# Expert retrieval of a streaming encoder step: separate gathers of U and V rows, two of nine tiles by a dense pass

## What is computed

```python
q = (xb @ w_query).reshape(PEER_BLOCK, PEER_HEADS, 2, D_HALF)
s = jnp.einsum('thpd,hpkd->thpk', q, sub_keys)
sv, si = lax.top_k(s, PEER_TOPK)                      # 16 of 128, twice per head
cand = sv[:, :, 0, :, None] + sv[:, :, 1, None, :]    # sums of pairs
cidx = si[:, :, 0, :, None] * N_KEYS + si[:, :, 1, None, :]
...
fv, fi = lax.top_k(cand, PEER_TOPK)                   # 16 experts per head
eidx = jnp.take_along_axis(cidx, fi, axis=-1)
g = jax.nn.softmax(fv, axis=-1)
a = jnp.einsum('thkd,td->thk', expert_u[eidx], xb)
w = g * jax.nn.gelu(a, approximate=False)
return jnp.einsum('thk,thkd->td', w, expert_v[eidx])
```

## Time and profile before

| what | value |
|---|---|
| median of 3 runs | 3683.47 us (3682.42 to 3684.99) |
| span of the profiled execution | 3684.3 us |
| PE busy | 3158.2 us, 86% |
| DVE busy | 2311.1 us, 63% |
| POOL busy | 1110.6 us, 30% |
| ACT busy | 719.1 us, 20% |
| gather queue | 1208.03 MB, 79.4% of 16 engines |

### The profile page before, as it was taken

The page is one execution under the profiler, slowest core; times in us unless marked ns, Lnnn a source line. Parts: engine busy times, 40 slices in busy tenths (PEclk is TensorE's granted clock), DMA queues, the critical chain, the costliest instruction groups (busy, mean ns, idle before and its releaser), DMA issues.

```text
span 3684.3 us, 48012 instructions
## 1 busy us (share of the span) xinstructions
PE 3158.2 (86%) x17895; PEld 1389.9 (38%) x17895; DVE 2311.1 (63%) x6107; ACT 719.1 (20%) x2373; POOL 1110.6 (30%) x1177
## 2 busy tenths in 40 slices
PE   6999999889888878988887898889788888977776
PEld 3545556634334324423432343344234334422222
DVE  1333343867757866775776677677667757765444
ACT  2434434311111111111111111111111111111111
POOL 0000000033333333333333333333333333333332
PEclk8999999799999999999999999999999999999999
DMA  5000114299999999999999999999999999999997
GB/s 217 24 29 23 35 34 169 91 401 421 421 421 419 418 414 417 413 414 420 415 414 420 416 414 415 417 418 416 412 417 416 416 416 418 413 414 420 419 418 326
DMA packets 192682, 1275.60 MB, mean 346 GB/s; under 512 B 21056, under 2 KB 24768, under 8 KB 44608
## 3 DMA queue, kind: packets, MB, share of 16 engines
q0 software_dynamic: 165888, 1208.03, 79.4%
q1 hardware_dynamic: 26560, 64.49, 4.9%
HBM read 1260.12 MB, written 12.32 MB: 345 GB/s over the span
## 4 chain that ended last, share of the span: by engine, by line
DMA 46%; PE 35%; DVE 9%; issue 5%; POOL 4%; ACT 1%; SPq 0%; DVEq 0%; POOLq 0%; ACTq 0%
DMA arena<-in_experts,arena 45%; PE PS L1353 10%; PE PS L1182 8%; PE PS L1367 7%; POOL arena L651 4%; DVE arena L976 4%; PE PS L1276 3%; PE PS L1166 2%; PE PS L1399 2%; PE PS L1265 1%; PE PS L1225 1%; DVE arena L1051 1%; DVE arena L1054 1%; DVE arena L1057 1%; PE PS L1205 0%
## 5 line engine op out<-in xcount | busy, mean ns | idle before, releaser
L1353 PE MATMUL PS<-arena 128*128 128x512 bf16 x6912 | 1655.6, 382 | 453.1 <-DVE arena L976 440.6
L976 DVE CUSTOM_DVE_ANT_0 arena<-arena,PS 128x1024 f32<-128x1024 f32 x1152 | 1396.2, 1221 | 871.7 <-DMA arena<-in_experts,arena 548.4
L651 POOL DMA_INDIRECT arena<-in_experts,arena x1152 | 1089.0, 945 | 1938.0 <-PE PS L1367 1572.7
L1353 PEld LDWEIGHTS PS<-arena 128*128 128x128 bf16 x6912 | 611.5, 98 | 1480.5 <-DVE arena L976 865.1
L1367 PE MATMUL PS<-arena 128*32 128x512 f32 x4608 | 558.8, 603 | 16.8 <-ACT arena L867 16.8
L861 ACT ACTIVATE arena<-arena 128x4 f32<-128x4 f32 x288 | 59.5, 207 | 2156.2 <-DVE arena L976 2137.0
L1182 PE MATMUL PS<-arena 128*128 128x512 f32 (+1 forms) x720 | 309.8, 567 | 13.9 <-DMA arena<-in_w_in 7.9
L1399 PEld LDWEIGHTS PS<-arena 128*128 128x128 f32 x2304 | 266.6, 192 | 101.5 <-issue 101.5
L1399 PE MATMUL PS<-arena 128*128 128x128 f32 x2304 | 289.7, 280 | 0.0
L867 ACT ACTIVATE arena<-arena 128x1 f32<-128x1 f32 x1152 | 245.5, 284 | 9.4
L1367 PEld LDWEIGHTS PS<-arena 128*32 128x32 f32 x4608 | 120.8, 109 | 313.9 <-issue 175.4
(11 more groups left out here) (124 smaller groups left out, 1526.8 us busy)
## 6 DMA issues: line engine op xcount, KB each, us to landing
arena<-in_experts,arena POOLq DMA_INDIRECT x1152
arena<-in_w_in SPq DMA_DIRECT2D x8, 1024.0 KB, 11.8
arena<-in_w_query SPq DMA_DIRECT2D x4, 2048.0 KB, 16.1
arena<-in_xT SPq DMA_DIRECT2D x9, 512.0 KB, 3.9
h_scratch<-arena SPq DMA_DIRECT2D x9, 512.0 KB, 2.9
arena<-h_scratch SPq DMA_DIRECT2D x9, 512.0 KB, 8.1
out<-arena SPq DMA_DIRECT2D x9, 512.0 KB
arena<-in_x_prompt SPq DMA_DIRECT2D x8, 512.0 KB, 3.5
```

The lines of the kernel that those rows point to most:

```text
L651: pool.indirect_dma_start(out=uv[r], out_offset=None, in_=experts, in_offset=bass.IndirectOffsetOnAxis(ap=expert_T[t % 2][:, tok:tok + 1], ...
L976: dve.tensor_tensor_reduce(uv[r][:, 0:D], uv[r][:, 0:D], xb(n), 1.0, 0.0, ALU.mult, ALU.add, a_dot[(n // 4) % 2][:, n % 4:n % 4 + 1]).then ...
L1353: mm = pe.matmul(PS[:, 2 + 2 * (n % 2) + c, :], pick[:, tok:tok + 1].broadcast_to([P, P]), parts[t % 2][k][:, 512 * c:512 * c + 512], star ...
```

## The change

The gathers of U and of V come apart, and 2 of 9 tiles no longer gather.

- **u rows by slot.** For the seven tiles 0 to 6, one gather takes the rows of U of one slot for all 128 tokens, a token per partition. x of the tile then lies as it is in SBUF (`xrow`), and `dot` reads it there; `spread_x` and the bf16 split are gone. 128 gathers of 4 KB rows per tile, in a ring of 8 (`u_ring`), each waiting for the dot that used its buffer.
- **v rows by token.** 128 gathers of 4 KB rows per tile in a ring of 8 (`e_ring`), one token each, 35 units (32 + LAG) behind the u gathers. The weights of a whole tile are gelu'd, gated, turned by TensorE once per tile; ScalarE writes four columns of `wz` in one instruction per unit.
- **Tiles 7 and 8 (`PAIR`) densely.** A gate matrix G (expert key i by token, per key j on the partitions) is written from one-hot rows: for four tokens VectorE writes `hot_j` (four instructions) and `hot_i` (one), TensorE multiplies them, ScalarE copies 256 columns into G. G holds half of the 128 i at a time, so there are two bursts of 64 groups, each over 4 units. Then 64 blocks follow over 47 units, twice: U^T and V of 128 experts are streamed in by SyncE (rings of 3), TensorE takes 8 products of 256 columns, ScalarE gelu, VectorE multiplies by G, and TensorE takes 4 products of 512 columns, two blocks behind.
- **Order.** Units 0 to 255 and 3 more; tile t + 1 is routed in 22 units, tile 1 from unit 0 and tiles 2 to 8 from unit 30 on, 16 units apart. First burst at units 151 to 154, blocks 155 to 201, second burst 202 to 205, blocks 206 to 252. x2 of the tiles is stored to DRAM and loaded again as rows.

```diff
-RING = 10
+D_TILES = (0, 1, 2, 3, 4, 5, 6)
+PAIR = (7, 8)
+UNITS = FOURS * PHASES
+U_RING, E_RING = 8, 8
+LAG = 3
+ROUTE_AT = (None, 0) + tuple(30 + 16 * r for r in range(7))
+DENSE_AT = ROUTE_AT[-1] + 25
+BURST_UNITS, BLOCK_UNITS = 4, 47
+T_RING = 3
...
+                for n in range(UNITS + LAG):
+                    s, f = split(n)
+                    if s < len(D_TILES):
...
+                            if m >= U_RING:
+                                pool.wait_ge(dots_ready, m - U_RING + 1)
+                            o = 4 * f + g
+                            pool.indirect_dma_start(
+                                out=u_ring[m % U_RING], out_offset=None, in_=expert_u,
+                                in_offset=bass.IndirectOffsetOnAxis(ap=eidx_u[s % 4][:, o:o + 1], axis=0))\
+                                .then_inc(u_in[m % U_RING], 16)
+                    v = n - FOURS - LAG
+                    if v >= 0:
...
+                        if v >= 2:
+                            pool.wait_ge(four_used, v - 1)
+                        for g in range(4):
+                            m, tok = 4 * v + g, 32 * g + f
+                            pool.indirect_dma_start(
+                                out=e_ring[m % E_RING], out_offset=None, in_=expert_v,
+                                in_offset=bass.IndirectOffsetOnAxis(ap=expert_T[s][:, tok:tok + 1], axis=0))\
+                                .then_inc(e_in[m % E_RING], 16)
...
+                def spots(j, g):
+                    n = GROUPS * j + g
+                    if n >= 2:
+                        dve.wait_ge(scatter_psum, n - 1)
+                    t0 = P * (g // FOURS) + 4 * (g % FOURS)
+                    for k in range(4):
+                        dve.tensor_scalar(hot_j[n % 2][:, k, :], iota, j_T[:, t0 + k:t0 + k + 1], g_T[:, t0 + k:t0 + k + 1],
+                                          ALU.is_equal, ALU.mult).then_inc(hot_ready, 1)
+                    dve.tensor_tensor(hot_i[n % 2], iota[:, HALF * j:HALF * (j + 1)].unsqueeze(1).broadcast_to([P, 4, HALF]),
+                                      i_T[:, t0:t0 + 4].unsqueeze(2).broadcast_to([P, 4, HALF]), ALU.is_equal).then_inc(hot_ready, 1)
+
+                def gate_dense(b):
+                    dve.wait_ge(act_ready, b + 1)
+                    dve.wait_ge(G_ready, GROUPS * (b // HALF + 1))
+                    if b >= W_RING:
+                        dve.wait_ge(dense_done, b - W_RING + 1)
...
+                def scatter(u, j, g):
...
+                    if n >= 2:
+                        pe.wait_ge(G_ready, n - 1)
...
+                    for k in range(4):
+                        mm = pe.matmul(PS[:, A_BANK + n % 2, HALF * k:HALF * k + HALF], hot_j[n % 2][:, k, :], hot_i[n % 2][:, k, :],
+                                       start=True, stop=True)
+                    mm.then_inc(scatter_psum, 1)
...
+                def dense_dots(b):
...
+                    pe.wait_ge(uT_in[b % T_RING], 16 * (b // T_RING + 1))
+                    for k in range(KD):
+                        mm = pe.matmul(PS[:, A_BANK, 0:2 * P], uT_ring[b % T_RING][:, k, :],
+                                       x2T_pair[:, k, :], start=(k == 0), stop=(k == KD - 1))
+                    mm.then_inc(act_psum, 1)
...
+                def dense_values(b):
...
+                    for q in range(2):
+                        for c in range(2):
+                            mm = pe.matmul(PS[:, ACC + 2 * q + c, :], w_ring[b % W_RING][:, P * q:P * q + P],
+                                           v_dense[b % T_RING][:, 512 * c:512 * c + 512], start=(b == 0), stop=(b == NKEYS - 1))
+                    mm.then_inc(dense_done, 1)
```

More of the change, by code:

```diff
@@ L48 @@
 SLOTS = H * TOPK
-RING = 10
-FIRST_BLOCK = 4
 QSP = 2
 FOURS = SLOTS // 4
-COLLECT_AT, SQUARES_AT, FINISH_AT = 0, 4, 5
-STEP_LENGTH = {"halves": 4, "sums": 6, "best": 3, "experts": 6}
[L60 to L69, removed]
-    pe, act, dve = {}, {}, {}
[L71 to L87, removed]
-    return pe, act, dve
@@ L100, with steps @@
-PE_EARLY = {30: [("x2T",)], 31: [("q", 0, 0)]}
-ACT_EARLY = {29: [("norm",)], 31: [("x2T",)]}
-DVE_EARLY = {29: [("norm",)]}
+D_TILES = (0, 1, 2, 3, 4, 5, 6)
+PAIR = (7, 8)
+PHASES = len(D_TILES) + 1
+UNITS = FOURS * PHASES
+U_RING, E_RING = 8, 8
+LAG = 3
+ROUTE_AT = (None, 0) + tuple(30 + 16 * r for r in range(7))
+STEP_LENGTH = {"halves": 4, "sums": 6, "best": 3, "experts": 6}
+def steps(k):
+    return [("halves", k, l) for l in range(4)] + [("sums", k), ("best", k, 0), ("experts", k, 0),
+                                                   ("best", k, 1), ("experts", k, 1)]
@@ new lines @@
+PE_AT, ACT_AT, DVE_AT = deal()
+DENSE_AT = ROUTE_AT[-1] + 25
+BURST_UNITS, BLOCK_UNITS = 4, 47
+GROUPS = 2 * P // 4
+HALF = NKEYS // 2
+DENSE = {}
+for j in range(2):
+    begin = DENSE_AT + j * (BURST_UNITS + BLOCK_UNITS)
+    for g in range(GROUPS):
+        DENSE.setdefault(begin + g * BURST_UNITS // GROUPS, []).append(("scatter", j, g))
+    for i in range(HALF):
+        DENSE.setdefault(begin + BURST_UNITS + i * BLOCK_UNITS // HALF, []).append(("block", j * HALF + i))
+DENSE_END = max(DENSE)
@@ new lines, with routes_before, weights_before, scatters_before @@
+assert DENSE_END < UNITS
+def routes_before(u):
+    return 1 + sum(ROUTE_AT[t] + 22 < u for t in range(1, NT))
+def weights_before(t):
+    return max(0, (ROUTE_AT[t] + 21) // FOURS)
+def scatters_before(u):
+    return sum(kind == "scatter" for at, events in DENSE.items() if at < u for kind, *_ in events)
+T_RING = 3
+ACT_RING, W_RING, BEHIND = 2, 4, 2
+ROUND = 12582912.0
+FINISH = D_TILES[:-1] + PAIR + D_TILES[-1:]
+COLLECT_AT = [FOURS * (s + 2) + LAG for s in range(len(D_TILES) - 1)] + [DENSE_END + 2] * 2 + [UNITS + LAG]
@@ new lines, in gelu, with spread_weights @@
+                def gelu(s):
+                    act.wait_ge(dots_ready, SLOTS * (s + 1))
+                    act.activation(a_dot[s % 2], a_dot[s % 2], ACT.Gelu).then_inc(gelu_ready, 1)
+                def spread_weights(v):
+                    s, f = split(v)
+                    if v == 0:
+                        act.wait_ge(zeros_ready, 2)
+                    if f == 0:
+                        act.wait_ge(wT_ready, s + 1)
+                    if v >= 2:
+                        act.wait_ge(four_used, v - 1)
+                    act.copy(wz[v % 2][:, :, 31:32], w_T[s % 2].rearrange("p (g f) -> p g f", g=4)[:, :, f:f + 1]).then_inc(wz_ready, 1)
```

673 lines of the change are left out of this document (430 added, 243 removed).

## The result

The changed kernel takes **3853.5 us** (3851.6 to 3862.1) where the kernel before took 3684.2: a ratio of 1.0464, interval 1.0449 to 1.0478. It is 4.6% slower and 43 us above the top of the predicted range.

What follows compares the result with a forecast made beforehand. Transferred bytes (DMA) were taken to set the time. 322 us saved were paid back by start, bursts, v tail, smaller rows, extra traffic and waits; the stages summed to 3688 us, 0.1% above before, range 3590 to 3810.

Steps and rivals of the forecast that it cites:

- 1.30 us for a 4 KB gather: Transfer time taken for one gather of 4 KB rows in the DMA-bound stages; eight make 10.4 us a unit.
- rival 1: DMA-bound stages: small rows stream as fast as large ones, 417 GB/s, giving 3605 us; chance 0.30.
- POOL's pitch of 1.245: Gather issue on POOL: unblocked gathers start 1.245 us apart, not shortened by half the bytes; eight cost 9.96 us.
- rival 4: Dense blocks: PE at half clock, 14 us a block, 1790 us in place of 1215, over 4200 in all; chance 2%.
- PSUM or SBUF as a source I price equally: Dots on DVE: reading the second operand from SBUF costs the same as from PSUM, four dots 4.6 us.
- rival 2: Units 35 to 150: POOL becomes the bound through waiting gathers, 11.1 us a unit, 3741 to about 3800 us; chance 0.25.
- a DMA share under 0.95: Profile sign for rival 2: DMA share under 0.95 while POOL's idle before a gather is only 0.30.
- the burst, 98 us, bounds 80 and 118: Each gate-matrix burst of 64 groups: 98 us, 80 if DVE overlaps better, 118 if PE is slow.
- the term of four one-hots: DVE's share of a burst group: four tensor_scalar of 128 columns at a pitch of 0.20 us.
- Rival 3: Bursts: PE's and ACT's turns don't overlap DVE's, 3.1 us a group, 198 a burst, 3888 total; 0.09 together with rival 4.
- Behind the last dot: End of the kernel: PE-bound v-only units 333 us, last six units 23 and the end 14; 370 in all.
- The allowance for lock step: POOL, DVE and PE waiting for one another in order: 1% of the three DMA-bound stages, 21 us, bounds 0 and 85.

Runs made afterwards that it cites:

- dots_psum: Changed kernel, but for tiles 0 to 3 ScalarE copies the x row to PSUM and the dots read it there: 3806.8 us, ratio 1.0328.
- experiment 3: Changed kernel with bursts spread over more units: both (burst_spread), 3835.7 us; both plus dots_psum and burst_double, 3793.6; first only, 3809.9; first only plus those two, 3741.2.
- burst_spread: Changed kernel with each of the two bursts spread over 16 units instead of 4, blocks over 35 instead of 47: 3835.7 us, ratio 1.0412.
- experiment 1: Where the dot's second operand lies: dots_psum, 3806.8 us; kernel before with its dot on two SBUF sources, 3684.0, or a plain product of two, 3675.1.
- burst_double: Changed kernel with the 64 needed columns of each burst product streamed twice, 128 wide: 3806.5 us (one run).

## Why the prediction was wrong, point by point

**Right.** The first dot at 740 (739). Units 35 to 66 came at 10.71 us against 10.65, at 404 GB/s: 1.30 us for a 4 KB gather held, rival 1 (417 GB/s) is dead. The fit of the Trainium skill, by which the prediction estimated 3.2 us for one such gather, was rightly kept out of the sum; it stands in "DMA: Bandwidth & Descriptors", section "Anatomy of one DMA — SWDGE (gpsimd) path", and only the rule of 1 MiB under Bandwidth. POOL's pitch of 1.245 for half the bytes held wherever no dot met a gather. A dot from SBUF takes DVE 1.22 us to run, as from PSUM. PE had nearly the full clock in the block stages (0.92) and all of it in the last stretch (1.00); rival 4 did not happen. The last stretch is PE's, 319 of 319 us busy at clock 1.00, and a block there is 7.0 us from start to start, as forecast:

```profile
3702.00 3.72 PE L1628 MATMUL PS<-arena 128*128 128x256 f32 x16
3705.56 3.60 PE L1641 MATMUL PS<-arena 128*128 128x512 f32 x8
3708.99 3.62 PE L1628 MATMUL PS<-arena 128*128 128x256 f32 x16
```

(The 3.72 and 3.60 overlap, so adding durations would say 7.3.) The idle DMA at the start, in the bursts and at the end is where I had put it.

**Wrong: "PSUM or SBUF as a source I price equally."** It is so for DVE and not for POOL. That one sentence costs 47 us by dots_psum (11 in units 0 to 34, 29 in units 35 to 150, the rest in the first burst and block stage), and, by the rows of experiment 3, most of what was left in the burst units of burst_spread. Of the 47 only some 34 fall in units whose dots were moved to PSUM; in units 128 to 150, where both kernels read SBUF, 6 us come from 179 gathers left to issue instead of 184, and the last 7 us were not traced. My rival 2 had the right bound, POOL, and the right price, 11.1 us a unit (units 67 to 150: 11.15), but for a reason that isn't there: it needed five of eight gathers to wait for semaphores, and the waits are 5 us in 930. That the number came out was luck. Its 0.23 us was the excess of the one gather of the earlier trace rows that had waited, and that gather had met an instruction with two SBUF sources, as shown in experiment 1; the 288 gathers of the kernel before that had waited over 0.5 us last 0.944 on the mean, the 864 others 0.946. So the effect that the failed step left out stood in the trace of the kernel before, and was read as the price of a wait. The arithmetic with the measured length closes: 8 x (1.08 + 0.30) = 11.04. I had also said that rival 2 would show as a DMA share under 0.95. The share hardly moved (1.02 and 1.01) and only the rate fell, 404 to 388 GB/s: the sign was badly chosen, GB/s is the one to read.

**Wrong: the burst, 98 us, bounds 80 and 118.** Both priced terms were low. On PE I took the full clock for the sum and half for the upper bound; half it was: 64 x 1.77 = 113 us, and four weighings of 3.64 and a wait of 10.2 us at the start bring 138 of the 143. The bound of 118 has 6 us for these two, which are 25. On DVE the term of four one-hots was 0.80 and is 1.11, worth 20 us a burst, visible only once PE is repaired. The burst costs 143 and 140: 87 us together, half the excess. DMA stood at a share of 0.46 meanwhile. Rival 3 (3.1 us a group by lost overlap) did not occur: a group is 2.2 us at most, and PE is busy 57 of 60.

**Off in size.** Behind the last dot 17 us were missing. The last block ends 342 us behind it where I had 333: 42 second halves and 39 first halves of blocks start in that time, one block more than my 39.5, and 30 weighings. From there to the end it is 45 us where I had 37; no run separates that. The block stages ran 18 us over the sum; in burst_double they are 11 us shorter (651 and 238), so most of it is what a long burst leaves behind; the other 7 were not tested. Units 0 to 34 keep 10 us over the sum even with the dots in PSUM, and units 35 to 150 keep 15; that is open too. The allowance for lock step, 21 us, had no place of its own in the trace: POOL's waits for others in units 67 to 150 are 5 us.

With the two failed steps sized as measured (47 for the source, 87 for the bursts less the 4 that overlap, no allowance) the sum would have been 3688 + 47 + 83 - 21 = 3797. The remaining 56 are 10 in units 0 to 34, 15 in units 35 to 150, 15 in the block stages and 17 at the end, less 1 at the start. So each of the two failed steps is larger than the 43 us by which the time left the range.

## What to carry to other kernels

Before an operand moves from PSUM to SBUF, look whether GpSimd issues gathers beside the instruction: the price is not in VectorE's own duration but in the gather's, and it is free only while POOL has slack. When a single row looks long (here 1.17 for 0.94), look what the other engines ran beside it before giving the excess to the wait in its brackets. Price an added instruction from a row with the same number of scalars and columns, and price a stage in which PE is the bound at both clock levels: here a burst of 64-column products had 0.50 where the blocks around it had 0.92 to 1.00. Work that an in-order bound will have to do at the end should start early: spreading a burst pays in a stage bound by transfers and costs where what comes behind it is TensorE's.
